# A recurrent unit's gate chains: two weight splits moved into each chain, the state's high and low parts made one pair later, and the last parts multiplied last

## What is computed

```
z = h @ w_in                                   # 1024 -> q, k, v, xr, yr, gate logits
c = causal_depthwise_conv(xr, conv_w, conv_b)  # 4 taps
gate_r = sigmoid(blocks(c) @ w_a + b_a);  gate_i = sigmoid(blocks(c) @ w_x + b_x)
log_a = -8 * gate_r * softplus(-rg_lambda);  a = exp(log_a)
u = sqrt(-expm1(2 * log_a)) * gate_i * c
h_t = a_t * h_{t-1} + u_t                      # a scan over 512 tokens
rnn = h * gelu(yr)                             # 1280 channels = 10 pieces of 128
merged = ... + sigmoid(gate logits) * (rnn @ w_br_rnn)
```

## Time and profile before

| | |
|---|---|
| median of 3 runs | 3262.33 us (3256.51 to 3262.58) |
| profiled execution, its own time | 3264.22 us |
| its span, first to last instruction | 3262.4 us |
| mean granted PE clock | 0.981 |
| PE matmul busy | 3144.4 us (96%) |
| DVE, ACT, POOL busy | 1783.2, 1162.1, 750.2 us |

### The profile page before, as it was taken

How to read it: one execution, slowest core, us unless ns; L and a number is a source line. 1 busy time by engine, 2 the same in 40 slices (tenths; PEclk the granted TensorE clock), 3 DMA queues, 4 the chain that set the end, 5 groups by cost and what they waited for, 6 DMA issues and landing times.

```text
span 3262.4 us, 35541 instructions
## 1 busy us (share of the span) xinstructions
PE 3144.4 (96%) x14196; PEld 2562.5 (79%) x14196; DVE 1783.2 (55%) x2997; ACT 1162.1 (36%) x1690; POOL 750.2 (23%) x455
## 2 busy tenths in 40 slices
PE   7979999899999999999999999999999999999998
PEld 5767777678888878888788888888888877788887
DVE  5554444567888883332555555555443466654442
ACT  4663444433233323333323222222332245532221
POOL 0000000031888888888000000002000120030000
PEclk9989999899999999999999999999999999999999
DMA  4225444324665667888755555552323331122321
GB/s 138 93 71 185 162 161 161 119 99 121 144 127 122 137 142 138 170 158 162 256 199 207 200 200 188 184 171 90 103 91 103 101 103 45 39 90 91 98 96 65
DMA packets 262485, 434.71 MB, mean 133 GB/s; under 512 B 135088, under 2 KB 138672, under 8 KB 261808
## 3 DMA queue, kind: packets, MB, share of 16 engines
q1 hardware_dynamic: 207024, 432.22, 40.8%
q0 software_dynamic: 55296, 0.22, 4.9%
HBM read 384.46 MB, written 81.46 MB: 143 GB/s over the span
## 4 chain that ended last, share of the span: by engine, by line
PE 79%; DVE 12%; ACT 6%; issue 1%; POOL 1%; DMA 0%; SPq 0%; POOLq 0%; ACTq 0%
PE pb L658 26%; PE pb L660 25%; PE pb L659 25%; ACT scr L1187 2%; DVE whl L1636 2%; DVE su L1862 1%; DVE ST L1863 1%; DVE su L1865 1%; ACT whl L1190 1%; DVE S L1636 1%; DVE ST L1636 1%; PE pb L930 1%; ACT L1187 1%; DVE sm L1864 1%; ACT S L1190 1%
## 5 line engine op out<-in xcount | busy, mean ns | idle before, releaser
L658 PE MATMUL pb<-H,whl 128*128 128x512 f32 x2416 | 977.4, 405 | 28.9 <-DVE whl L1636 12.5
L659 PE MATMUL pb<-H,whl 128*128 128x512 f32 x2416 | 950.8, 394 | 0.0
L660 PE MATMUL pb<-H,whl 128*128 128x512 f32 x2416 | 950.6, 393 | 0.0
L1636 DVE TENSOR_TENSOR whl<-raw,whl 128x1024 fp32r<-128x1024 f32 (+4 forms) x554 | 651.5, 1192 | 521.1 <-ACT whl L1190 519.7
L1190 ACT ACTIVATE whl<-raw 128x1024 fp32r<-128x1024 f32 (+4 forms) x554 | 546.8, 1003 | 457.6 <-PE pb L660 457.1
L658 PE MATMUL pb<-S,whl 128*128 128x512 f32 (+1 forms) x1716 | 673.2, 392 | 23.8 <-DVE whl L1636 11.7
L2203 POOL DMA_INDIRECT gd<-scr,place x384 | 642.4, 1673 | 202.5 <-issue 114.9
L660 PE MATMUL pb<-S,whl 128*128 128x512 f32 (+1 forms) x1716 | 668.9, 390 | 0.0
L659 PE MATMUL pb<-S,whl 128*128 128x512 f32 (+1 forms) x1716 | 668.9, 390 | 0.0
L658 PEld LDWEIGHTS pb<-H,whl 128*128 128x128 f32 x2416 | 459.6, 190 | 130.4 <-DVE whl L1636 13.7
L660 PEld LDWEIGHTS pb<-H,whl 128*128 128x128 f32 x2416 | 459.4, 190 | 100.1
(11 more groups left out here) (198 smaller groups left out, 2330.4 us busy)
## 6 DMA issues: line engine op xcount, KB each, us to landing
raw<-in_pu SPq DMA_DIRECT2D x128, 512.0 KB, 3.8
raw<-in_pv SPq DMA_DIRECT2D x128, 512.0 KB, 4.4
raw<-in_w_in SPq DMA_DIRECT2D x72, 512.0 KB, 3.8
ad<-scr SPq DMA_DIRECT2D x128, 256.0 KB, 4.1
GA<-gd SPq DMA_DIRECT2D x60, 512.0 KB, 4.6
GA<-ad SPq DMA_DIRECT2D x60, 512.0 KB, 6.3
raw<-in_wg SPq DMA_DIRECT2D x44, 512.0 KB, 3.3
raw<-in_wu SPq DMA_DIRECT2D x44, 512.0 KB, 4.3
```

The costliest lines, as they stand in the source:

```text
L658: e.matmul(o, lh, h, start=start, stop=False, skip_group_check=True)
L659: e.matmul(o, lh, l, start=False, stop=False, skip_group_check=True)
L660: return e.matmul(o, ll, h, start=False, stop=stop, skip_group_check=True)
L1636: return e.tensor_tensor(o, x, y, op)
```

## The change

Three edits. First, in `rnn_gates` ACT and DVE both cut two more units (`split(q.j + NW)`) in the middle of the chain: ACT ahead of the exponentials, DVE ahead of the second group of products. Second, `rh` (ACT) and `rl` (DVE) of a pair are no longer made at the end of its chain but in the next turn: ACT behind the `pad` copy of the next piece, DVE inside `conv4`; for the last two pairs behind the following unit splits. Third, PE takes the second halves for m = 0, 1, 2 in two steps: states 5, 6, 7 for all three, then states 8 and 9 for all three.

```diff
@@ tensor: recurrence
-                for m in range(8):
+                second = [("rnn", 5 + c) for c in range(5)]
+                begun = [q.unit("w_brr", 2 * m + 1) for m in range(3)]
+                for ks, done in ((range(3), False), (range(3, 5), True)):
+                    for m, j in enumerate(begun):
+                        linear(j, bank[m], rh[5:10], rl[5:10], second, ("brr", m) if done else None, ks, 5, start=False)
+                for m in range(3, 8):
@@ scalar: rnn_gates, behind the tanh of both pieces, ahead of the exps
+                split(q.j + NW)
@@ scalar: rnn_gates, behind Sqrt
+
+            def rnn_high(pair):
+                for c in pair:
                     q.wait_ge(dve, ("rnn_out", c))
                     copy(rh[c], rlf[c]).then_inc(act.up(("rnn_hi", c)), 1)
@@ scalar: recurrence
                         copy(pad[i][:, 32:544], bank[i]).then_inc(act.up(("xr_raw", d)), 1)
+                        if d in (4, 6, 8):
+                            rnn_high((d - 4, d - 3))
                         q.wait_ge(dve, ("conv", d))
...
                 for m in range(4):
                     weights("w_brr", 2 * m)
+                rnn_high((6, 7))
                 rnn_gates((8, 9))
+                rnn_high((8, 9))
@@ vector: conv4(c, beside), between the last tap and conv_parts
+                rnn_low(beside)
@@ vector: rnn_gates, at its end
+
+            def rnn_low(pair):
                 for c in pair:
                     q.wait_ge(act, ("rnn_hi", c))
                     tt(rl[c], rlf[c], f(rh[c]), ALU.subtract).then_inc(dve.up(("rnn", c)), 1)
@@ vector: recurrence
-                        conv4(d)
+                        conv4(d, (d - 4, d - 3) if d in (4, 6, 8) else ())
...
+                rnn_low((6, 7))
                 rnn_gates((8, 9))
+                rnn_low((8, 9))
```

More of the change, by code:

```diff
@@ L753, in recurrence @@
                 gates_of_rnn(7)
-                for m in range(8):
+                second = [("rnn", 5 + c) for c in range(5)]
[4 more added lines that the diff above has]
+                for m in range(3, 8):
                     if m > 3:
                         first_half(m)
-                    linear(q.unit("w_brr", 2 * m + 1), bank[m % 4], rh[5:10], rl[5:10],
-                           [("rnn", 5 + c) for c in range(5)], ("brr", m), range(5), 5, start=False)
+                    linear(q.unit("w_brr", 2 * m + 1), bank[m % 4], rh[5:10], rl[5:10], second, ("brr", m), range(5), 5,
+                           start=False)
             def first_attention():
@@ L1699, in scalars, with conv4 @@
                 ts(nsp, sq[3], -8.0, ALU.mult).then_inc(dve.up("softplus"), 1)
-            def conv4(c):
+            def conv4(c, beside=()):
                 i, cv, w = c % 2, rhf[c], [prm("conv_w", 4 * c + j) for j in range(4)]
```

## The result

| | before | changed |
|---|---|---|
| median | 3262.45 us (4 runs, 3256.51 to 3263.58) | **3238.81 us** (4 runs, 3237.95 to 3240.74) |
| profiled execution, own time | 3264.22 us | 3239.58 us |
| its span | 3262.4 us | 3237.7 us |
| mean granted PE clock | 0.981 | 0.983 |

The ratio to before is 0.9932, 95% interval 0.9915 to 0.9949. The forecast was 3240.8 us, with a range of 3235 to 3250.

What follows compares the result with a forecast made beforehand. PE was taken to bound the kernel, losing 30.6 us to waits and low clock. 18.0 us up to merge gate 6 + 4.55 at the last products - 1.0 low clock = 21.5 us, giving 3240.8 us, range 3235 to 3250.

Steps and rivals of the forecast that it cites:

- The bound and the ceiling: PE from 86.84 to 244.46 us loses 30.6 us to waits and low clock, all the change can win.
- Splits in the chain: Units cut ahead of the exps delay the roots by 0.95 to 1.9 us; waits ahead of units 15, 23, 31 go.
- The turn's slack: ScalarE's own turn of 34.3 us fits PE's 35.4 us with 1.1 us to spare.
- The chain from 155 to 206 us: ScalarE's and VectorE's alone: PE starts unit 34 at 185.0 us after waiting 2.9, then loses 1.8 us twice.
- Rival 1: ScalarE's turn outlasts PE's, so PE waits in two turns; gain 8 to 19 us, about 3249 us; chance 0.16.
- Last parts last: Last products, states 8 and 9: no wait for state 9; 2.64 us wait and 1.75 low clock go, 4.55 us.
- Low clock behind the short waits: Matmuls behind the two new waits near 203 and 206 us may run slow; 1.0 us taken off the gain.
- Rule on banks: Skill's rule that cycling through banks lowers PE's clock; by it the 45 matmuls through three banks would be slow.
- rival 2: 45 matmuls that change banks run at 0.427 instead of 0.227 us, costing 9 us; 3250 us; chance 0.03.
- Rival 3: High-part copies behind the tanh wait for their loads and hold up the chain; slower, 3271 us; chance 0.03.
- Behind the stretch: After 245 us nothing is tied to clock time, so a gain before it arrives whole at the end.
- Rival 4: Gained time is returned behind 245 us, where a later stage could wait for a transfer; 3262 us; chance 0.04.

Runs made afterwards that it cites:

- both ends: Changed kernel with a shorter end chain (piece 9's convolution parts, unit 39, states' parts of 6 and 7 moved), nothing left out; ratio 0.9913, once more 0.9918.
- Parts only: Kernel before with the second edit alone, the states' high and low parts made a pair later; ratio 0.9937, 15.8 us won between first gate and branch products.
- splits only: Kernel before with the first edit alone, two more units cut inside each chain on ScalarE and VectorE; ratio 0.9976.
- filler: Changed kernel with two more ScalarE copies (1.9 us together) in every chain, into memory that nothing reads; ratio 0.9949.

## Why the prediction was right, and where it was not

- **The bound and the ceiling** (30.6 us between the first gate products and the branch product, all else PE's steady step): right. With both ends all but 3.0 us of it came back.
- **The three waits ahead of units 15, 23, 31:** they went, but the prediction gave them to the wrong edit ("Splits in the chain ... The three waits ahead of units 15, 23 and 31 go"). Parts only removes them without a split, splits only trades them for others. This is the step that failed. That the sum came out all the same is luck in part: with all three edits in place each wait goes once, whichever edit it is put to, and the sum had counted each once.
- **The turn's slack** (34.3 against 35.4, 1.1 us): 1.00 and 0.99 us in the trace, and the filler used it up. ScalarE's own turn was 34.3 us in the forecast and 34.36 in the trace (97.22 to 132.58, less 1.00).
- **The chain from 155 to 206 us:** unit 34 at 185.0 forecast, 184.65 measured; wait 2.9, 2.85; the two short waits at 203.35 and 206.5, measured 202.88 and 206.16. The execution began 0.4 us early, so each start is right within 0.1; the two short waits were to cost 1.8 us each and cost 1.5 and 1.8. Rival 1 lived on this chain and fell.
- **Last parts last:** no wait for state 9, right. "In the old order ... lost about 4": 3.6 with the hidden end, and 1.7 of low clock, in the run without this edit. What the prediction didn't say is that this edit needs the splits: without them unit 43 is late.
- **Low clock behind the short waits**, 1.0 us taken of 0.14 to 1.95: 0.1 in this execution, which is luck. The changed kernel's other profiled execution shows the other end. Both rows give length, busy of PE, PEld, DVE, ACT, POOL and then PE's clock, from just ahead of the wait near 203 us; first the changed kernel,

```profile
202.00:221.00 19.00, 16.50 (x71) 13.36 (x72) 13.47 (x18) 15.34 (x21) 0.00 (x0) 1.00 0.41 132
```

  then the same kernel once more:

```profile
203.00:222.00 19.00, 17.12 (x62) 13.43 (x63) 13.46 (x18) 15.34 (x21) 0.00 (x0) 0.82 0.41 132
```

  Clock 1.00 and 0.82 for the same instructions, and 20.4 us won instead of 22.4. The two short waits of that execution were

```profile
203.89 0.50 PE L658 MATMUL pb<-S,whl 128*128 128x512 f32 x1 [2.99 <-DVE whl L1649]
...
207.16 0.79 PE L658 MATMUL pb<-H,whl 128*128 128x512 f32 x1 [0.99 <-ACT scr L1192]
```

  The first is 1.6 us longer than in the other execution (1.37) because PE came to it earlier: of the 66 steps ahead of it, the ones behind the start of unit 34, the first execution had 1.7 us of low clock and this one 0.1. Low clock ahead of a wait only shortens the wait, and in both executions merge gate 6 starts 122.44 us behind the first gate product. Behind merge gate 6 it is added to the time: 0.1 us in the first execution, 2.15 in this one. So the term was a draw. Its upper bound was somewhat low: 2.15 us here, and 2.75 behind the wait of 4.18 us in the run of the last edit alone. What decides where the low clock falls stays open.
- **Rule on banks** (rival 2): the 45 matmuls that go through three banks keep the step of 0.2267 us. The prediction had read a rule by which they would be slow out of the Trainium skill (TensorE: Matmul & The Clock Gate, "A second HAM failure mode: psum-queue depth-cycling"). What the section tells is that a kernel that cycled through banks left PE short idles between its groups of matmuls, and its clock fell and rose. Here these 45 matmuls have no idle between them and the granted clock from 217 to 227 us is 1.00: the change of banks alone slows nothing, and no run here shows the case that the section tells of.
- **Rival 3** (copies held up by their loads): ScalarE shows no idle time ahead of the two copies in any of the five chains; in the first the copies follow the tanh at once:

```profile
89.30 0.74 ACT L1192 ACTIVATE scr<-scr,sm 128x512 f32<-128x512 f32 x1
89.91 2.02 ACT L1195 ACTIVATE whl<-raw 128x1024 fp32r<-128x1024 f32 x2
```

- **Behind the stretch:** the prediction said that a gain arrives whole. Spans differ by 24.7 us: 0.4 from before the stretch, 22.4 in it, and 1.9 behind. Of the 1.9, 1.5 lie in attention's first head, where before PE waited 1.54 us for VectorE and then ran slow:

```profile
300.98 0.32 PE L658 MATMUL pb<-S 64*128 64x128 f32 x1 [1.54 <-DVE S L1636]
...
303.34 0.63 PE L658 MATMUL pb<-H,whl 128*128 128x512 f32 x1
```

  In the changed kernel the low clock came a little earlier, ahead of that product; PE reached it later and found the state there:

```profile
275.72 0.63 PE L658 MATMUL pb<-H,whl 128*128 128x512 f32 x1
276.15 0.63 PE L659 MATMUL pb<-H,whl 128*128 128x512 f32 x1
```

  Both have clock 0.79 over 8 us there. It is no effect of the shift by 22 us: from the first `pb<-ST,cst` matmul to the first `pb<-cst,ST` matmul the changed kernel took 12.16 us in one execution and 13.03 in the other, before took 13.67, and both ends, which is shifted by still more, 13.50 and 13.67. Given 15 us of spread behind the stretch I count the 1.9 to the spread. Rival 4 fell as well: behind 245 us PE waits at the same places in both kernels, 69.7 us in all before and 67.7 changed.

## What to carry to other kernels

When a fast engine waits for operands that slower in-order engines prepare, ask first what stands in their queues ahead of the preparation without anyone waiting for it, and move that back; here this gave 15.8 us by itself, of the 22.4 that all three edits give, and 10.6 when added last (11.8 to 22.4). Preparing operands earlier lengthens the chain in which it is put and pays only as far as that chain has slack against the fast engine's turn (here 1.0 us of 35.4), so work out both turns. And an order that helps by asking for one thing later asks for another earlier: the same three products in two steps cost 2.3 us in the stretch alone (1.3 without the low clock behind) and gained 5.4 beside the edit that had the next weights ready.

## What was not expected of the hardware

What a wait of PE costs beyond itself is not fixed by its length. In the trace of before PE waits 2.57 us for the low part of a unit at 105.89 us and again, one turn later, at 144.42 us. The 156 steps behind the first take 0.4 us more than at the steady step, the 156 behind the second 1.7 us more. The waits, and then 8 us from just ahead of each restart (length, busy of PE, PEld, DVE, ACT, POOL, then PE's clock):

```profile
105.89 0.50 PE L658 MATMUL pb<-H,whl 128*128 128x512 f32 x1 [2.57 <-DVE whl L1636]
...
144.42 0.50 PE L658 MATMUL pb<-H,whl 128*128 128x512 f32 x1 [2.57 <-DVE whl L1636]
```

```profile
105.00:113.00 8.00, 7.09 (x30) 5.57 (x31) 5.47 (x7) 4.34 (x6) 0.00 (x0) 1.00 0.25 75
144.00:152.00 8.00, 7.58 (x26) 6.11 (x27) 5.31 (x8) 4.75 (x6) 0.00 (x0) 0.79 0.28 83
```

The changed kernel shows the same in its two executions with 0.1 and 2.15 us behind merge gate 6, though there the waits ahead differ too (1.37 and 1.63 us, 2.99 and 0.99). And where the low clock falls on matmuls ahead of a product that would have to wait anyway, it costs nothing, since the wait is shorter by as much: 1.7 us ahead of the wait at 202.88 us were taken up in this way.
